# A token's four expert rows fetched as one piece and summed by tile, in a one-core MoE step on Trainium2

## What is computed

```python
h = rmsnorm(x)                                   # 320 x 1024
top_v, top_e = top_k(h @ w_router + b_router, 4)
gate = softmax(top_v)                            # 4 gates of a token
for each token t and rank r:                     # expert e = top_e[t, r]
    gu = h[t] @ w_gu[e] + b_gu[e]                # 1024 -> 2048
    gt, up = min(gu[:1024], 7), clip(gu[1024:], -7, 7)
    act = gt * sigmoid(1.702 * gt) * (up + 1)
    x[t] += gate[t, r] * (act @ w_dn[e] + b_dn[e])
y = x * rsqrt(mean(x*x) + 1e-5) * norm_final
```

## Time and profile before

| | |
|---|---|
| time, median of 3 runs | 1360.25 us (1359.26 to 1362.63) |
| the profiled execution: its time, its span | 1359.06 us, 1357.3 us |
| PE busy, DVE busy, ACT busy | 93%, 34%, 17% of the span |
| DMA moved | 479.33 MB, 353 GB/s over the span |
| mean granted TensorE clock | 0.991 |

### The profile page before, as it was taken

One profiled execution on the slowest core, in us unless ns is written; L12 is line 12 of the kernel. 1 busy time (PEld: TensorE's weight loads), 2 busy tenths in 40 slices (PEclk: granted clock), 3 DMA queues, 4 the chain that ended last, 5 costly groups with the idle time before them and its releaser, 6 DMA issues.

```text
span 1357.3 us, 14397 instructions
## 1 busy us (share of the span) xinstructions
PE 1263.5 (93%) x5895; PEld 570.5 (42%) x5895; DVE 458.9 (34%) x808; ACT 230.5 (17%) x333; POOL 116.9 (9%) x154
## 2 busy tenths in 40 slices
PE   7999999999999999999999999999987788878785
PEld 5756766666543333333333333333332223222231
DVE  2898322311463322223113313222422222233226
ACT  4112432210221111111011111111211111111121
POOL 1110100000010100000000000100011000000020
PEclk9999999999999999999999999999999999999898
DMA  9715826464699999999999999999999999999994
GB/s 332 256 63 143 268 87 152 159 248 191 252 367 424 426 425 426 427 426 426 426 425 426 427 426 427 423 427 426 425 426 425 425 425 426 426 425 427 423 389 153
DMA packets 97399, 479.33 MB, mean 353 GB/s; under 512 B 44163, under 2 KB 46339, under 8 KB 72595
## 3 DMA queue, kind: packets, MB, share of 16 engines
q1 hardware_dynamic: 84641, 459.36, 83.3%
q0 software_dynamic: 10672, 15.39, 3.3%
q10 hardware_dynamic: 1994, 3.25, 0.7%
HBM read 477.57 MB, written 22.61 MB: 369 GB/s over the span
## 4 chain that ended last, share of the span: by engine, by line
PE 70%; DMA 27%; issue 1%; DVE 1%; ACT 0%; POOL 0%; SPq 0%; POOLq 0%; DVEq 0%; ACTq 0%
PE PS L1753 27%; PE PS L1391 15%; PE PS L1786 13%; DMA ring<-in_w_gu 11%; DMA ring<-in_w_dn 10%; PE PS L1571 4%; PE PS L1333 4%; PE PS L1615 3%; DMA arena<-in_w_dn 2%; DMA ring<-y_rows 2%; PE PS L1427 2%; DMA ring<-in_w_in 1%; DMA y_rows<-arena 1%; DVE XX L1314 0%; PE PS L1658 0%
## 5 line engine op out<-in xcount | busy, mean ns | idle before, releaser
L1753 PE MATMUL PS<-ring,arena 128*64 128x512 f32 x1824 | 406.7, 598 | 38.6 <-DMA ring<-in_w_gu 26.7
L1244 DVE TENSOR_TENSOR arena<-PS,XX 128x1024 f32<-128x1024 f32 x32 | 39.2, 1225 | 660.4 <-PE PS L1753 660.4
L1753 PEld LDWEIGHTS PS<-ring,arena 128*64 128x64 f32 x1824 | 129.8, 139 | 293.4 <-issue 290.9
L1786 PE MATMUL PS<-ring,arena 128*64 128x512 f32 x896 | 202.2, 600 | 15.4 <-DMA ring<-in_w_dn 14.4
L1391 PE MATMUL PS<-arena,ring 128*128 128x320 f32 x768 | 213.5, 434 | 0.6 <-DMA ring<-in_w_in 0.6
L1391 PEld LDWEIGHTS PS<-arena,ring 128*128 128x128 f32 x768 | 144.1, 190 | 59.3 <-issue 2.0
L1753 PE MATMUL PS<-arena 128*64 128x512 f32 x608 | 136.3, 595 | 12.2 <-DMA arena<-in_w_gu 11.4
L852 ACT ACTIVATE arena<-arena 128x1024 f32<-128x1024 f32 x32 | 33.8, 1057 | 619.4 <-DVE arena L1247 619.4
L542 POOL DMA_INDIRECT y_rows<-arena x60 | 59.6, 994 | 792.9 <-ACT arena L833 783.7
L1786 PEld LDWEIGHTS PS<-ring,arena 128*64 128x64 f32 x896 | 61.7, 138 | 139.5 <-issue 139.5
L1333 PEld LDWEIGHTS PS<-ident,arena 128*128 128x128 f32 (+3 forms) x580 | 63.1, 142 | 55.7 <-issue 43.1
(11 more groups left out here) (206 smaller groups left out, 663.7 us busy)
## 6 DMA issues: line engine op xcount, KB each, us to landing
ring<-in_w_gu SPq DMA_DIRECT2D x96, 2048.0 KB, 27.3
ring<-in_w_dn SPq DMA_DIRECT2D x48, 2048.0 KB, 28.7
arena<-in_w_gu SPq DMA_DIRECT2D x31, 2048.0 KB, 28.5
arena<-in_w_dn SPq DMA_DIRECT2D x16, 2048.0 KB, 30.4
ring<-in_w_in SPq DMA_DIRECT2D x11, 2048.0 KB, 11.8
ring<-in_w_mem_kv SPq DMA_DIRECT2D x2, 2048.0 KB, 20.1
ring<-in_cache_mem_k SPq DMA_DIRECT2D x32, 128.0 KB, 3.4
ring<-in_cache_mem_v SPq DMA_DIRECT2D x4, 1024.0 KB, 6.2
```

The source lines that it names most:

```text
L1244: nc.vector.tensor_tensor(gbuf[:], PS[:, 0:2, :], g_bias, ALU.add).then_inc(main["g_added"], 1)
L1753: last = mm(PS[64 * h:64 * h + 64, 2 * g + b, :], in_block(xT[:, k, :], b), (spare[kk] if m == BONUS else moe_ring(m, 2)[:, kk]) [:, g * D ...
L1786: last = mm(PS[64 * h:64 * h + 64, 4 + b, :], actT[:, b, j, c * BLK:(c + 1) * BLK], moe_ring(m, 4)[:, j, h * 512:(h + 1) * 512], start=c = ...
```

## The change

Three things are changed together.

1. `y_rows` is ordered by token: row 4*t + r holds rank r of token t (`worth` on GpSimd holds the new numbers), so a token's four ranks are 16 KB in one piece. `rank_rows(tt)` reads a tile of tokens with one DMA, 128, 128 and 64 pieces of 16 KB, three DMAs in place of eight. The first two are issued when expert 29 has been scattered, the third when (31,2) has been used. All four ranks are zeroed in the mixer (5 MB in place of 2.5). VectorE adds tile by tile, the four ranks of a tile after each other.
2. On TensorE `bias_sum(2)` and `to_tokens(0,0)` go ahead of `down(31)` chunk 4, and `to_tokens(0,1)` and `to_tokens(0,2)` ahead of `down(31)` chunk 5.
3. `norm_final` is no longer read into 128 partitions. ScalarE's queue reads its halves early, as two rows of 2 KB, and after `to_tokens(1,2)` TensorE multiplies a column of ones by them (`spread_norm`, two products into PSUM banks 4 and 5). VectorE reads it from there.

```diff
-RANK_PLACES = [PLACE[-10], PLACE[-9], PLACE[-6], PLACE[-5]]
+RANK_PLACES = [PLACE[-10], PLACE[-9], PLACE[-6]]
...
+    y_tokens = y_rows.rearrange("(t r) d -> t r d", r=TOPK)
...
-    def yr(r):
-        return room(RANK_PLACES[r]).rearrange("p (t n) -> p t n", t=4)[:, 0:TT, :]
-
-    normfin = room(RANK_PLACES[0]).rearrange("p (t n) -> p t n", t=4)[:, TT, :]
+    def yr(tt):
+        return room(RANK_PLACES[tt]).rearrange("p (r n) -> p r n", r=TOPK)
+
+    nrow = XN[:, 1, 512:D]
+    normfin = PS[:, 4:6, :].rearrange("p a b -> p (a b)")
...
-                sp.dma_start(y_rows[2 * T:4 * T, :].rearrange("(p j) c -> p (j c)", p=P).rearrange("p (n c) -> p n c", c=512),
-                             W[0].rearrange("p b t -> p (b t)")[:, None, 0:512].to_broadcast([P, 10, 512])) \
+                sp.dma_start(y_rows.rearrange("(p j) c -> p (j c)", p=P).rearrange("p (n c) -> p n c", c=512),
+                             W[0].rearrange("p b t -> p (b t)")[:, None, 0:512].to_broadcast([P, 20, 512])) \
...
-        sp.wait_ge(main["dn_done"], NE - 2)
-        sp.dma_start(normfin, a["norm_final"].partition_broadcast(P)).then_inc(fin_in, 16)
...
-        def rank_rows(r):
-            nc.gpsimd.dma_start(yr(r)[:, 0:2, :], y_rows[r * T:r * T + 2 * P, :].rearrange("(t p) d -> p t d", p=P)) \
-                .then_inc(yr_in[r], 16)
-            nc.gpsimd.dma_start(yr(r)[0:ROWS[2], 2, :], y_rows[r * T + 2 * P:(r + 1) * T, :]).then_inc(yr_in[r], 16)
+        def rank_rows(tt):
+            r = ROWS[tt]
+            nc.gpsimd.dma_start(yr(tt)[0:r], y_tokens[tt * P:tt * P + r]).then_inc(yr_in[tt], 16)
...
-        pool.wait_ge(main["scattered"], 32 * (DIRECT[0] - 1))
+        pool.wait_ge(main["scattered"], 32 * DIRECT[0])
         rank_rows(0)
-        pool.wait_ge(main["scattered"], 32 * DIRECT[0])
         rank_rows(1)
         pool.wait_ge(main[consumed(RINGED[-6])[0]], consumed(RINGED[-6])[2])
         rank_rows(2)
-        pool.wait_ge(main["gu_done"], NE)
-        rank_rows(3)
...
+            act.dma_start(nrow[64 + 32 * h:65 + 32 * h, :], a["norm_final"][512 * h:512 * (h + 1)][None, :]).then_inc(fin_in, 16)
...
-        for r in range(TOPK):
-            j = TOPK - 1 - r
-            dve.wait_ge(yr_in[r], 32)
-            for tt in range(TT):
-                n = ROWS[tt]
+        for tt in range(TT):
+            n = ROWS[tt]
+            dve.wait_ge(yr_in[tt], 16)
+            for r in range(TOPK):
+                j = TOPK - 1 - r
...
-        dve.wait_ge(fin_in, 16)
+        dve.wait_ge(norm_spread, 1)
         last_norm(0)
...
         def amid_last():
-            bias_sum(2, False)
-            to_tokens(0, 0)
+            to_tokens(0, 1)
+            to_tokens(0, 2)
...
             pe.wait_ge(main["actT_ready"], NE)
+            bias_sum(2, False)
             pe.wait_ge(main["zs_ready"], NE - 1)
+            to_tokens(0, 0)
             down(0, e, amid_last)
-            to_tokens(0, 1)
-            to_tokens(0, 2)
             pe.wait_ge(main["zs_ready"], NE)
             for tt in range(TT):
                 to_tokens(1, tt).then_inc(bd_done, 1)
+            spread_norm()
+
+        def spread_norm():
+            pe.wait_ge(fin_in, 32)
+            for h in range(2):
+                last = mm(PS[:, 4 + h, :], ones[64 + 32 * h:65 + 32 * h, :], nrow[64 + 32 * h:65 + 32 * h, :],
+                          start=True, stop=True)
+            last.then_inc(norm_spread, 1)
```

More of the change, by code:

```diff
@@ L280, in program @@
         sem(s) for s in ("bdn_in", "dense_ready", "gt_done", "gt_ready", "bd_done", "bd_added"))
-    yr_in = [sem(f"yr_in{i}") for i in range(TOPK)]
-    fin_in, fin_out = sem("fin_in"), sem("fin_out")
+    yr_in = [sem(f"yr_in{tt}") for tt in range(TT)]
+    fin_in, fin_out, norm_spread = sem("fin_in"), sem("fin_out"), sem("norm_spread")
     zeroed, hot_made, w_turned, w_copied = sem("zeroed"), sem("hot_made"), sem("w_turned"), sem("w_copied")
@@ L493, in _ @@
                        allow_small_or_imprecise_dtypes=True)
-        nc.gpsimd.iota(worth[:, :, :, 1], [[2 * P, TT], [-2 * T, TOPK]], base=2 * T * (TOPK - 1) - SKIP,
-                       channel_multiplier=2, allow_small_or_imprecise_dtypes=True).then_inc(consts, 1)
+        nc.gpsimd.iota(worth[:, :, :, 1], [[2 * TOPK * P, TT], [-2, TOPK]], base=2 * (TOPK - 1) - SKIP,
+                       channel_multiplier=2 * TOPK, allow_small_or_imprecise_dtypes=True).then_inc(consts, 1)
         for a6 in range(2):
@@ L1271, in add_products @@
             dve.wait_ge(bd_done, tt + 1)
-            dve.wait_ge(summed, (TOPK - 1) * TT + tt + 1)
+            dve.wait_ge(summed, TOPK * (tt + 1))
             if tt < 2:
@@ L1305, in _ @@
         dve.nop()
-        for r in range(TOPK):
-            j = TOPK - 1 - r
-            dve.wait_ge(yr_in[r], 32)
-            for tt in range(TT):
-                n = ROWS[tt]
+        for tt in range(TT):
[3 more added lines that the diff above has]
+                j = TOPK - 1 - r
                 if r:
-                    dve.wait_ge(summed, (r - 1) * TT + tt + 1)
-                nc.vector.scalar_tensor_tensor(X[0:n, tt, :], yr(r)[0:n, tt, :], gates[0:n, tt, j:j + 1], X[0:n, tt, :],
+                    dve.wait_ge(summed, TOPK * tt + r)
+                nc.vector.scalar_tensor_tensor(X[0:n, tt, :], yr(tt)[0:n, r, :], gates[0:n, tt, j:j + 1], X[0:n, tt, :],
                                                ALU.mult, ALU.add).then_inc(summed, 1)
@@ L1931, in _ @@
                 over_window(2)
+                pe.wait_ge(main["zs_ready"], 3 * NE)
                 pe.nop()
@@ L1934, in _ @@
                 bias_sum(tt, True).then_inc(bd_done, 1)
+            pe.wait_ge(main["zs_ready"], 2 * NE)
+            spread_norm()
             pe.nop()
```

## The result

The changed kernel takes 1369.57 us (median of 12 runs, 1367.08 to 1376.8), the kernel before, measured beside it, 1361.5 us (12 runs). The ratio is 1.0062, with a 95% interval of 1.0048 to 1.0077. The forecast was 1361.5 us, within 1355 to 1366: no change. The measured time is outside that range, on the slow side. The profiled execution took 1368.81 us with a span of 1367.1 us.

The account below looks back on a forecast made before the run. Two chains, TensorE's and VectorE's sums, share DMA engines at the end: weights lose 6.4 us, VectorE's sums leave the path, TensorE's tail gives 2.6 less 1.1. Span 1358.6 plus 2.95 makes 1361.5 us, range 1355 to 1366.

Parts of the forecast that it names:

- What bounds the end, and who gets the engines: Last 55 us: TensorE's and VectorE's chains end almost together, fed by the same DMA engines, which take queues' pieces in turn.
- the 4 KB rival: Software queue keeps 4 KB pieces, weights keep their share, rows come late: 1358.5 us; chance 0.14.
- The price of a pair: One weight piece plus one 16 KB row piece on a DMA engine: 1.236 us instead of 0.782.
- The backlog of weights at 1304 us: Latest DMA engine: 6.5 pieces of (30,4) left at 1304.1 us, and 24 more for the next three chunks.
- The crowding of the third tile: Row DMA to 64 partitions near the end: adds from nothing to some 2.5 us, taken as 0.3 us.
- The moved products and the norm: TensorE's tail: 2.6 us won by earlier token products, less 1.07 us (0.5 to 2) for spread_norm.
- C1: Start of down(31) chunk 5 on TensorE: 1331.67 us before, forecast 1338.1 us.
- N: Start of last_norm(0): 1348.15 us before, forecast 1349.5 us, with 9.15 us from there to the end.
- The zeroing: 2.5 MB more zeroed in the mixer: costed at 0, up to 9 us without the cover of later work.
- The clock: Rival: TensorE's clock falls in the longer wait before down(31) chunk 4; low for 7 us or more, 1365.5 us; chance 0.12.
- C0: Start of down(31) chunk 4 on TensorE: 1324.30 us before, forecast 1330.7 us.
- the main case: Weights late as summed, sharing engines with 16 KB row pieces: 1361.5 us, own range 1359 to 1364.5; chance 0.52.

Follow-up runs that it names:

- the second profile: The changed kernel itself, run and profiled again without any edit; ratio 1.0073 to the kernel before.
- the run on 128 partitions: The changed kernel with the third tile read over 128 partitions, 64 more rows of zeros (1 MB more); ratio 1.0013 to the kernel before.
- the second run: The kernel before with only the change's TensorE order and spread norm, rows by rank as before; ratio 0.9993.
- 4 KB pieces: The changed kernel with y_rows by rank again, so each tile's DMA reads four rows of 4 KB for a token; ratio 1.0020 to the kernel before.
- rows behind the weights: The changed kernel with SP issuing the three row DMAs on the weights' queue, behind the last chunk, none by GpSimd; ratio 1.0015 to the kernel before.
- third tile first: The changed kernel with SP issuing rows on the weights' queue behind the last chunk, tiles read and summed 2, 0, 1; ratio 1.0018 to the kernel before.
- two queues: The changed kernel over 128 partitions, first tile issued by GpSimd, the others behind the weights on their queue; ratio 1.0002 to the kernel before.

## Why the prediction was wrong, step by step

**What bounds the end, and who gets the engines: right.** Two chains, and the weights pay for faster rows. Pieces are 16 KB on the software queue, so the 4 KB rival is out. The Trainium skill ("DMA: Bandwidth & Descriptors", SWDGE vs HWDGE vs iDMA) gives a packet of the software queue as 4096 B or less by preference. This trace differs: 2.24 MB went in 153 packets. The price of a pair was right to 0.1 us: from (30,4) to (30,5) 9.80 us against 9.9.

**The backlog of weights at 1304 us: off by two pieces.** My steps put down(30) chunk 4 at 1310.6; it started at 1313.07, and at 1311.72 in the second profile. The first row pieces moved at 1306 us in the first profile, as I had taken, and at 1305 in the second (by my steps 0.5 us), so the rest is the backlog. I had read it from one execution, and it was off by 0.6 to 2.5 us.

**The crowding of the third tile: the step that failed.** I wrote that it "can add from nothing to some 2.5 us", and took 0.3. It added 14.26 - 9.87 = 4.4 us, 5.0 in the second profile, and the run on 128 partitions takes it away. I had read its price from the queue between 1334 and 1340 us of the kernel before (0.174 us a piece). But the weights had ended and the engines were only 43% taken there; that fewer engines at work crowd each other less is my guess, which no run tests. I had also doubled only the four row pieces of an engine: the weight pieces beside them slowed as much (1.05 us). The stretch to read was 1316 to 1324 us, where the weights still flowed and a piece took 0.85 us. The Trainium skill offers a reason ("SBUF — State Buffer", Door 1: The DMA port swizzle): partitions 0 to 63 lie behind half of the 16 ports. The runs agree with it (0.62 us a piece on 128 partitions, 1.0 on 64), though they don't show the ports themselves.

**The moved products and the norm: right.** From C1 to N it was 11.45 us against 11.4, and from N to the end 9.2 against 9.15. VectorE's sums left the path as forecast. The zeroing cost nothing: TensorE's first products of expert 0 start between 379.4 and 381.7 us in all profiles, with no order by the bytes zeroed (381.1 with 2.5 MB in the second run, 379.7 with 5 MB in the last).

**The clock: named, but as a rival of its own.** I gave it 0.12, as if it stood beside the late weights. It came with them: in both profiles of the changed kernel the blocks behind waits of 4.03 to 6.17 us took 5.35 to 5.62 us, those behind 1.50 and 1.54 us took 3.65. The changed kernel's windows (busy times, granted clock, DMA share, GB/s) show 1.00 while nothing had waited long, and 0.59 behind the wait of 5.58 us:

```profile
1306.00:1312.00 6.00, 3.02 (x16) 0.72 (x10) 2.86 (x3) 0.00 (x0) 0.00 (x0) 1.00 1.00 419
1337.00:1342.00 5.00, 4.87 (x14) 1.52 (x16) 3.41 (x3) 0.00 (x0) 0.00 (x0) 0.59 0.22 88
```

The block took 2.0 us more.

**The sum.** N came 8.4 us after the forecast 1349.5: 6.4 us in C0 (2.5 backlog, 4.1 crowding beyond the 0.3 taken, less 0.2 of rounding in the pairs and the wait) and 2.0 us of the slow block. In the main case's own bounds C0 could be no later than 1333.5, so its range was as wrong as its middle. Slower by over 0.3% had 0.22.

**What stays open.** Whether a held clock would give back its 2 us, and why the backlog of the latest engine differs by some pieces between executions.

## What to carry to other kernels

Making a second stream's pieces as large as those of the main stream can double what the second stream takes from the engines that serve both (24.4% to 53.3% here); if the main stream is what the end waits for, put the second one behind it on the same queue. Here a DMA to only 64 of 128 partitions slowed everything that was in flight with it, so it can be faster to move more bytes over all partitions (1 MB on top of 5.24 here, a fifth). Read the price of such crowding where the other stream is still running, not where it has ended.

## What the runs showed of the hardware that was not expected

- A transfer to 64 partitions raised the price of a 16 KB piece from 0.62 us to 1.0 to 1.15 us, for its own pieces and for the weights' alike, and it did so on either queue. Behind the weights with the third tile last (1324 to 1328 us), then with it first (1312 to 1316 us):

```profile
q1 hardware_dynamic: 62, 0.87, 84.8%
```

```profile
q1 hardware_dynamic: 71, 1.00, 109.6%
```

  That is 0.848 x 64 / 53 = 1.02 us and 1.096 x 64 / 61 = 1.15 us a piece.
- A wait of 4.05 us with the rows taking turns was followed by a block of 5.35 us in three profiles, while 3.48 us ahead of 1262.29 us, in the changed kernel's timeline, was followed by 48 products in 12.22 us:

```profile
1262.29 12.22 PE L1750 MATMUL PS<-ring,arena 128*64 128x512 f32 x48 [3.48 <-issue]
```

  At 3.65 us for 16 that would be 10.95, so a shorter wait cost 1.3 us there.
- The length of a wait alone did not decide the clock. The wait of 2.04 us ahead of `bias_sum(2)` was followed by a to_tokens(0,0) of 1.99 us in both profiles of the changed kernel, and by 3.22 to 3.64 us in four of the variants (4 KB pieces, rows behind the weights, third tile first, two queues), with a mean granted clock of 0.50 to 0.64 in the stretch.
- Products that filled the wait kept the block at 3.65 us, and no measurable time was won.
